# A rearranged front for a hybrid layer kernel: half of the modulation unsplit, the projection begun on four channel blocks

## The reference

```python
mod = silu(cond) @ w_ada + b_ada            # 1024 x 6144, one row per token group
shift_a, scale_a, gate_a, shift_f, scale_f, gate_f = split(mod, 6)
h = rmsnorm(x) * norm_mix_g * (1 + scale_a) + shift_a      # x + position embedding for latents
q, k, v, g, za_f, za_b, u = split(h @ w_in)                # 2080 columns
la = log_sigmoid(za @ w_a_up + b_a) / 16                   # rank 16, one per direction
... bidirectional gated linear attention, mean pooling, @ w_out, residual with gate_a
h = rmsnorm(x) * norm_ffn_g * (1 + scale_f) + shift_f
x = x + gate_f * expert_choice_moe(h)                      # 16 experts, 80 rows each
```

## Time and profile before

| what | us |
|---|---|
| median of 3 runs (lowest, highest) | 1917.02 (1916.72, 1923.43) |
| the profiled execution, its own time | 1916.14 |
| its span, first to last instruction | 1914.3 |
| TensorE busy in the span | 1839.0 (96%) |
| VectorE, ScalarE busy | 1559.4, 1257.9 |
| DMA over the span | 326 GB/s |

### The profile page before, as it was taken

One profiled execution on the slowest core, in us unless ns is written; L12 is line 12 of the kernel. 1 busy time (PEld: TensorE's weight loads), 2 busy tenths in 40 slices (PEclk: granted clock), 3 DMA queues, 4 the chain that ended last, 5 costly groups with the idle time before them and its releaser, 6 DMA issues.

```text
span 1914.3 us, 25062 instructions
## 1 busy us (share of the span) xinstructions
PE 1839.0 (96%) x9064; PEld 1506.5 (79%) x9064; DVE 1559.4 (81%) x1254; ACT 1257.9 (66%) x1005; POOL 272.9 (14%) x118
## 2 busy tenths in 40 slices
PE   3899788999999999999999999999999999999998
PEld 2678666758888888888888888888888888888886
DVE  5531855589898989889898989898989898989897
ACT  5342643257777777767676767676767676777774
POOL 1000000010021211212030303030303030303060
PEclk9999998999999999999999999999999999999999
DMA  9422442579999999999999999999999999999993
GB/s 360 138 63 75 155 151 95 186 276 389 388 386 388 385 385 385 371 384 375 384 377 385 369 385 375 387 370 389 370 386 377 384 368 387 374 384 369 391 378 126
DMA packets 281021, 624.61 MB, mean 326 GB/s; under 512 B 12454, under 2 KB 45851, under 8 KB 280987
## 3 DMA queue, kind: packets, MB, share of 16 engines
q1 hardware_dynamic: 273690, 598.75, 85.2%
q0 software_dynamic: 6000, 20.68, 3.7%
q10 hardware_dynamic: 1296, 4.72, 0.6%
HBM read 608.97 MB, written 15.14 MB: 326 GB/s over the span
## 4 chain that ended last, share of the span: by engine, by line
PE 92%; DVE 4%; ACT 2%; DMA 1%; issue 1%; SPq 0%; ACTq 0%; DVEq 0%
PE bank L1728 17%; PE bank L1729 17%; PE bank L1732 17%; PE bank L1758 8%; PE bank L1754 8%; PE bank L1753 8%; PE bank L1349 3%; PE bank L1350 3%; PE bank L1351 3%; PE bank L1738 1%; DMA raw<-in_w_ada 1%; DVE w_lo L907 1%; ACT w_hi L620 1%; PE bank L1382 1%; PE bank L1558 1%
## 5 line engine op out<-in xcount | busy, mean ns | idle before, releaser
L1211 DVE TENSOR_TENSOR w_lo<-raw,w_hi 128x2048 fp32r<-128x2048 f32 x528 | 1197.9, 2289 | 121.5 <-ACT w_hi L807 119.5
L807 ACT CAST w_hi<-raw 128x2048 fp32r<-128x2048 f32 x524 | 998.0, 1914 | 181.0 <-PE bank L1732 104.2
L1728 PE MATMUL bank<-w_hi,xe_hi 128*128 128x512 f32 (+1 forms) x1536 | 573.8, 380 | 0.0
L1729 PE MATMUL bank<-w_hi,xe_lo 128*128 128x512 f32 (+1 forms) x1536 | 563.4, 373 | 0.0
L1732 PE MATMUL bank<-w_lo,xe_hi 128*128 128x512 f32 (+1 forms) x1536 | 380.4, 373 | 0.0
L1728 PEld LDWEIGHTS bank<-w_hi,xe_hi 128*128 128x128 f32 x1536 | 290.0, 189 | 49.5 <-issue 1.7
L1729 PEld LDWEIGHTS bank<-w_hi,xe_lo 128*128 128x128 f32 x1536 | 290.3, 189 | 48.5
L1732 PEld LDWEIGHTS bank<-w_lo,xe_hi 128*128 128x128 f32 x1536 | 273.4, 189 | 51.8
L1754 PE MATMUL bank<-w_hi,hT_lo 128*128 128x512 f32 x700 | 273.0, 390 | 0.0
L1753 PE MATMUL bank<-w_hi,hT_hi 128*128 128x512 f32 x700 | 272.7, 390 | 0.0
L573 POOL DMA_INDIRECT acc_dram<-yrow,idx_s x15 | 43.6, 2909 | 1072.6 <-DVE yrow L1253 1072.6
(11 more groups left out here) (250 smaller groups left out, 1366.5 us busy)
## 6 DMA issues: line engine op xcount, KB each, us to landing
raw<-in_w_e_gate SPq DMA_DIRECT2D x176, 1024.0 KB, 11.3
raw<-in_w_e_up SPq DMA_DIRECT2D x176, 1024.0 KB, 11.5
raw<-in_w_e_down SPq DMA_DIRECT2D x176, 1024.0 KB, 11.1
raw<-in_w_ada SPq DMA_DIRECT2D x20, 1024.0 KB, 5.4
raw<-in_w_in SPq DMA_DIRECT2D x8, 1024.0 KB, 5.3
raw<-in_w_out SPq DMA_DIRECT2D x4, 1024.0 KB, 5.0
ada_raw<-in_w_ada SPq DMA_DIRECT2D x4, 1024.0 KB, 12.1
acc_dram<-x POOLq DMA_DIRECT2D x5, 512.0 KB, 2.9
```

The costliest lines, as they stand in the source:

```text
L807: nc.scalar.copy(hi_slot(j), raw[:, raw_slot(j), :]).then_inc(hi_done, 1)
L1211: nc.vector.tensor_tensor(lo_slot(j), raw[:, raw_slot(j), :], hi_slot(j), ALU.subtract).then_inc(lo_done, 1)
L1728: nc.tensor.matmul(out, xe_hi[:, kk, :], wh[:, k, :], start=kk == 0, stop=False)
L1729: nc.tensor.matmul(out, xe_lo[:, kk, :], wh[:, k, :], start=False, stop=False)
```

## The change

It changes what happens before and in the first column block. Blocks 0 and 2 of w_ada (the first half of shift and of scale) are loaded ahead of everything else, to places of their own, and multiplied without a split, in plain fp32 with the two columns of silu (`ada_unsplit`). The first unit of w_in comes right behind them. Scale and shift for channel blocks 0 to 3 are then enough to start the projection on these; w_ada blocks 1 and 3, split as before, stand between the first four channel blocks, and blocks 4 to 7 follow. The position rows shrink to one table of 8 rows, spread over the tokens by a matmul with a selection matrix, and one table of 128 rows, added as it is. ScalarE's queue loads the identity and three of the vectors. The decay weights' two parts stand side by side in `wza_both`, so that one product with the rounded h gives both; the up-projection gets its rows twice. The diff, cut to its core; in the rest, `hT_hi` and `hT_lo` become two halves of one tensor (`hT_part`), semaphores are shared, and a few counts follow:

```diff
-PRE = [("ada", b, kh) for b in range(ADA_FIRST) for kh in range(2)]
...
+ADA_ORDER = (0, 2, 1, 3)
+PRE = [("ada", b, kh) for b in ADA_ORDER[2:] for kh in range(2)]
...
-WIN0 = len(PRE)
-PRE += [("win", b, kh) for b in range(4) for kh in range(2)]
...
+WIN0 = len(PRE) - 1
+PRE += [("win", b, kh) for b in range(4) for kh in range(2)][1:]
...
-FRONT = 2 * ADA_FIRST
+FRONT_SLOTS = (0, 1, 6, 7)
+FRONT = len(FRONT_SLOTS)
+W0_SLOT = 2
...
-    return n if n < FRONT else (n - FRONT) % PRE_RING
+    return FRONT_SLOTS[n] if n < FRONT else (n - FRONT) % PRE_RING
...
-        pos_sb = at("pos_sb", [P, T_LAT, D], F32, DR + 20 * KB)
+        ada_f = [at(f"ada_f{q}", [P, UNIT], F32, SPL + (q % 2 * SPLIT + q // 2) * UNIT * 4) for q in range(4)]
+        pos_col = at("pos_col", [P, 512], F32, SPL + 40 * KB)
+        pos_row = at("pos_row", [8, 512], F32, SPL + 42 * KB)
+        pos_sel = at("pos_sel", [8, 8, GRID_W], F32, SPL + 44 * KB)
+        w0_hi = at("w0_hi", [P, UNIT], F32R, DR)
+        w0_lo = at("w0_lo", [P, UNIT], F32R, DR + 8 * KB)
...
+        hT_split = at("hT_split", [P, 2, 2, KD // 2, NTOK], F32R, HT)
...
-            for row, v, n in ((V_C, c[0], KD), (V_CCTX, c_ctx, KD), (V_BADA, b_ada[0], 48),
-                              (V_GMIX, norm_mix_g[0], KD), (V_GFFN, norm_ffn_g[0], KD),
-                              (V_GGLA, gla_norm_g[0], 1), (V_PSC, pool_scale[0], 4)):
+            for row, v, n in ((V_C, c[0], KD), (V_CCTX, c_ctx, KD), (V_BADA, b_ada[0], 48), (V_GMIX, norm_mix_g[0], KD)):
                 load(vecs[row:row + n, :], v.rearrange("(k p) -> k p", p=P), vec_in)
-            load(const[:, :], consts, const_in)
+            for q in range(4):
+                b, kh = ADA_ORDER[q // 2], q % 2
+                load(ada_f[q].rearrange("p (k n) -> p k n", k=4), rows(w_ada[0, kh * 512:(kh + 1) * 512, b * 512:(b + 1) * 512]), ada_in[q])
+            load(raw[:, W0_SLOT, :].rearrange("p (k n) -> p k n", k=4), rows(w_in[0, 0:512, WIN_BLOCKS[0]:WIN_BLOCKS[0] + 512]), w0_in)
             for n in range(NPRE):
                 if n >= FRONT:
-                    last = [q for q in range(n) if pre_slot(q) == pre_slot(n)][-1]
-                    sp.wait_ge(lo_done, last + 1)
+                    last = [q for q in range(n) if pre_slot(q) == pre_slot(n)]
+                    if last:
+                        sp.wait_ge(lo_done, last[-1] + 1)
+                    else:
+                        sp.wait_ge(w0_l, 1)
                 load(raw[:, pre_slot(n), :].rearrange("p (k n) -> p k n", k=4), pre_source(n),
                      raw_full[pre_slot(n)])
...
+                    load(const[:, P:K_COLS], consts[:, P:K_COLS], const_in)
...
+            for r in range(0, 4 * RANK, 2 * RANK):
+                pool.dma_start(wup[r:r + RANK, 0:hw], w_a_up_f[0]).then_inc(up_in, 16)
+                pool.dma_start(wup[r + RANK:r + 2 * RANK, hw:2 * hw], w_a_up_b[0]).then_inc(up_in, 16)
...
+                elif u < SPLIT:
+                    act.wait_ge(ada_f_ps, 2)
+                    act.wait_ge(x_pos, T_LAT)
...
+            act.dma_start(const[:, 0:P], consts[:, 0:P]).then_inc(id_in, 16)
+            for row, v, k in ((V_GFFN, norm_ffn_g[0], KD), (V_GGLA, gla_norm_g[0], 1), (V_PSC, pool_scale[0], 4)):
+                act.dma_start(vecs[row:row + k, :], v.rearrange("(k p) -> k p", p=P)).then_inc(vec_in, 16)
+            tokens(0)
+            act.dma_start(pos_row[:, :], pos.rearrange("(r c) d -> r c d", c=GRID_W)[:, 0, 0:512]).then_inc(pos_in, 16)
+            act.dma_start(pos_col[:, :], pos[0:P, 512:D]).then_inc(pos_in, 16)
+            for t in range(1, TILES):
                 tokens(t)
...
+                q = place_of(b)
+                if q < 2:
+                    act.wait_ge(ada_f_ps, q + 1)
+                else:
+                    act.wait_ge(unit_used, ada_unit(b) + 2)
+                    act.wait_ge(mod_ps, q - 1)
+                m = 2 if q < 2 else 4
+                nc.scalar.copy(modrow[0:m, q % 2, :], ada_bank(b)[0:m, :]).then_inc(mod_row, 1)
...
+            square(0)
+            square(1)
+            turned(0)
+            square(2)
+            turned(1)
+            square(3)
+            mod_rows(0)
+            turned(2)
+            square(4)
+            turned(3)
+            act.wait_ge(xT_ps, 2 * T_LAT)
+            act.wait_ge(w0_in, 16)
+            nc.scalar.copy(w0_hi[:, :], raw[:, W0_SLOT, :]).then_inc(w0_h, 1)
+            turned(4)
+            mod_rows(2)
+            high_row(0)
+            high_row(1)
             high(0)
             high(1)
-            square(0)
+            high_row(2)
+            high_row(3)
             high(2)
-            mod_rows(0)
-            square(1)
-            high(3)
-            square(2)
-            high(4)
-            mod_rows(1)
-            square(3)
-            turned(0)
-            high(5)
-            square(4)
-            turned(1)
-            turned(2)
-            high(6)
-            mod_rows(2)
-            turned(3)
-            high(7)
-            high(8)
-            turned(4)
             act.wait_ge(small_in, 48)
             nc.scalar.copy(wza_hi[:, :, 0:2 * RANK], wza[:, :, :]).then_inc(wza_h, 1)
+            nc.scalar.copy(wza_both[:, :, 0:2 * RANK], wza[:, :, :]).then_inc(wza_h, 1)
+            high(3)
+            mod_rows(1)
+            high(4)
             mod_rows(3)
...
+            for k in range(4, KD):
+                high_row(k)
+                if k == 5:
+                    high(5)
...
             def place(t):
-                dve.wait_ge(x_in[t], 32)
-                nc.vector.tensor_tensor(x_all[:, t, :], x_all[:, t, :], pos_sb[:, t, :], ALU.add).then_inc(x_pos, 1)
+                dve.wait_ge(tile_in[t], 16)
+                dve.wait_ge(pos_ps, t + 1)
+                nc.vector.tensor_tensor(x_all[:, t, 0:512], x_all[:, t, 0:512], bank[4 + t % 2 * 2][:, :], ALU.add).then_inc(x_row, 1)
+                dve.wait_ge(pos_in, 32)
+                nc.vector.tensor_tensor(x_all[:, t, 512:D], x_all[:, t, 512:D], pos_col[:, :], ALU.add).then_inc(x_pos, 1)
...
+                at_ = place_of(b)
+                dve.wait_ge(mod_ps, at_ + 1)
+                if at_ >= 1:
+                    dve.wait_ge(mod_done, at_ + (b >= ADA_FIRST))
...
+                if at_ < 2:
+                    nc.vector.tensor_tensor(modT[:, 4 * b:4 * b + 4, :], q[:, :, 0:2], bias, ALU.add).then_inc(mod_done, 1)
+                    return
...
+            dve.wait_ge(id_in, 16)
+            nc.vector.tensor_copy(pos_sel[:, :, :], ident[0:8, 0:8].unsqueeze(2).broadcast_to([8, 8, GRID_W])).then_inc(pos_set, 1)
...
+            def scale_rows(half):
+                ks = slice(4 * half, 4 * half + 4)
+                dve.wait_ge(mod_done, 2 * half + 2)
+                gm = vecT[:, V_GMIX + 4 * half:V_GMIX + 4 * half + 4].unsqueeze(2).broadcast_to([P, 4, 2])
+                nc.vector.scalar_tensor_tensor(out=scaleA[:, ks, :], in0=modT[:, 8 + 4 * half:12 + 4 * half, :], scalar=1.0, in1=gm, op0=ALU.add, op1=ALU.mult).then_inc(
+                    scaled if half == 0 else mod_done, 1)
+                if half == 0:
+                    dve.wait_ge(scaled, 1)
+                else:
+                    dve.wait_ge(mod_done, ADA_FIRST + 1)
...
+            def low_row(k):
+                dve.wait_ge(h_hi, k + 1)
+                nc.vector.tensor_tensor(hT_part(1, k), hT[:, k, :], hT_part(0, k), ALU.subtract).then_inc(h_lo, 1)
+            place(0)
+            norm(0)
+            place(1)
+            norm(1)
+            turned(0)
+            place(2)
+            norm(2)
+            turned(1)
+            place(3)
+            norm(3)
+            turned(2)
+            mod_columns(0)
+            norm(4)
+            turned(3)
+            dve.wait_ge(w0_h, 1)
+            nc.vector.tensor_tensor(w0_lo[:, :], raw[:, W0_SLOT, :], w0_hi[:, :], ALU.subtract).then_inc(w0_l, 1)
+            turned(4)
+            mod_columns(2)
+            scale_rows(0)
+            dve.wait_ge(xT_act, TILES)
+            dve.wait_ge(xT_dve, TILES)
             modulated(0)
-            dve.wait_ge(wza_h, 1)
-            nc.vector.tensor_tensor(wza_lo[:, :, 0:2 * RANK], wza[:, :, :], wza_hi[:, :, 0:2 * RANK], ALU.subtract).then_inc(wza_l, 1)
-            for k in range(KD):
-                if k + 1 < KD:
-                    modulated(k + 1)
-                dve.wait_ge(h_hi, k + 1)
-                nc.vector.tensor_tensor(hT_lo[:, k, :], hT[:, k, :], hT_hi[:, k, :], ALU.subtract).then_inc(h_lo, 1)
-                if k in (3, 6):
-                    low(8 + k // 3)
+            modulated(1)
+            low_row(0)
+            modulated(2)
+            low_row(1)
+            low(0)
+            modulated(3)
+            low(1)
+            low_row(2)
+            low_row(3)
+            low(2)
+            dve.wait_ge(wza_h, 2)
```

(89 more changed lines are left out.)

142 lines of the change are left out of this document (39 added, 103 removed).

## The result

The kernel after takes 1903.08 us (median of 5 runs, 1901.39 to 1907.02), beside 1917.08 us for the kernel before on the same chip (5 runs, 1916.72 to 1923.43). The ratio is 0.9923, with a 95% interval of 0.9906 to 0.9939: faster by 0.6 to 0.9%. The forecast was 1901 us, range 1895 to 1910. The profiled execution took 1903.08 us with a span of 1901.3, 13.0 less than the 1914.3 before.

The account below looks back on a forecast made before the run. TensorE bounds the kernel, so the front adds one for one: first block at 42.6 us, plus 42.4 and 0.9, is 85.9 against 101.7, 15.8 gained; 1916.14 becomes 1900.3, 0.9 up to the median, given as 1901 us, range 1895 to 1910.

Parts of the forecast that it names:

- the front alone decides, and what is behind it keeps its length: Before the second column block: 15.8 us gained; from there to the end the same 1812 us as before.
- rival E: In the experts: the front is shorter but they give it back, total 1917 us; chance 0.04.
- D: In the front: SyncE's units land late, free up to 17.5 us; at 25 us, total 1907; chance 0.05.
- F: In the front: a pause behind each ScalarE table load, three in all, total 1905 us; chance 0.02.
- G: Small loads behind 9.5 MB land late, costing from 54 us on, 1927 at 80; expected landing 39; chance 0.03.
- The wait ahead of channel block 4: In the first column block: TensorE waits 0.8 to 1.1 us for the last scale rows.
- the landing of the column table: In the front: 262 KB, issued at about 3, lands at 7.5 us without a wait; at 11 adds 3.2.
- the first unsplit half: In the front: first half block of unsplit w_ada takes 4.4 us, to 21.9, with 3.3 us at half rate.
- the half rate of the first projection block: In the first column block: half clock adds 1.7 us to a sum of 42.4.
- The 65-row decay weights cost TensorE nothing by rows.: In the up-projection: 512 columns stream whatever the rows are; no cost, bounds 0 and 5 x 1.05 us.

Follow-up runs that it names:

- The run with the tables first: Kernel after with the two small position loads ahead of three vector loads and the first tile of x in ScalarE's queue; median 1901.49 us, ratio 0.9902.
- the other order: Kernel after, small tables kept, with all four places and squares ahead of the first copy to hT; median 1901.76 us, ratio 0.9904.
- pipelined: Kernel after with small tables loaded first and each place issued ahead of the norm of the tile before; median 1897.69 us, ratio 0.9884.
- the warmed kernel: Kernel after with 18 more identity products on TensorE before the position products; median 1904.02 us, ratio 0.9912.
- the kernel with three decay products: Kernel after with the decay rows back in three products and 33 rows; median 1907.30 us, ratio 0.9942.
- the one with full rows: Kernel after with 2.1 MB of position rows loaded again, no position products, all places ahead of the first copy to hT; median 1896.57 us, ratio 0.9890.

## Why the prediction was right, and where it was off

**Right: the front alone decides, and what is behind it keeps its length.** The stages behind 190 us moved as a whole (last rows 1896.7 to 1883.7, 13.0), so rival E, the gain given back by the experts, didn't occur. Neither did D (TensorE waits for no unit of w_ada in the front), F (in the kernel after too silu follows its table load by 0.01 us), nor G: the small loads were issued at 25.48 and took 12.6, landing at 38.1 where I had 39. The wait ahead of channel block 4 was 0.70 us by TensorE's own idle time, and I had given it 0.8 to 1.1.

**Off by 2.2: the landing of the column table.** The step "Issued at about 3 it lands at 7.5 and nobody waits" failed. I took the 5.0 us of the first position load, issued at 1.18. The row is that of the second, issued at 2.14, and says 8.7; the third, issued at 3.34, took 11.4. This 256 KB load, issued at 3.17, took 6.67, while 330 GB/s were moved: ahead of it in its own queue stood 592 KB, and SyncE's first unit was issued at 2.27 where before it was 3.61. My own bound, 3.2 us for a landing at 11, was nearer than the 7.5 of the sum. Place 0 ended its first half at 12.76 in place of about 10.5. The run with the tables first gave 1.8 us back, which shows this cause.

**Off by 1.5: the first unsplit half.** "The first half block takes 4.4" took 5.84 in the chain, since half rate went on for longer than the 3.3 us of the earlier trace rows. I had used one measured duration of a state as if it were a constant, and the trace of before had others, in its own front:

```profile
42.34 1.06 PE L1402 MATMUL bank<-const,xn 128*128 128x128 f32 x8 [2.61 <-ACT hT L643]
...
45.98 1.94 PE L1402 MATMUL bank<-const,xn 128*128 128x128 f32 x8 [2.25 <-ACT hT L643]
```

The eight turns take 1.06 us behind a pause of 2.61 and 1.94 behind a shorter one of 2.25. From 45.98 half rate goes on to 51.34, 5.4 us at a granted clock of 0.51. By 25.7 us I was 3.8 behind, and every later step kept that distance or lost a little of it (28.8 became 32.48, 42.6 became 46.15). Two kernels with an unchanged product give 1.0 of the 1.5 back by a shorter half rate (4.92 us with the other order, 4.89 pipelined). Whether full clock all through would bring the whole 1.5 back was not shown: the warmed kernel lost its clock again before it.

**Off by 0.9: the half rate of the first projection block.** I added 1.7 us for it; by the chain's rows, 13 products and a part took 5.84 us (46.15 to 51.99) where 14 x 0.23 is 3.2, so 2.6. The region was 44.2 long in place of 43.3. (The same sum for the kernel before, given as 36.7, adds up to 36.5; from 65.10 to 101.53 it was 36.43.)

**Off by 1.9 the other way: "The 65-row decay weights cost TensorE nothing by rows."** The bounds that I gave, 0 and 5 x 1.05, pointed upward, and excluded a gain for no reason that the rows gave. The cost was in the trace of before: the product after the one at 104.41 in the earlier trace rows starts 1.05 us behind it, where two unsplit instructions of 0.443 are 0.89, and it is itself 0.32 behind the one ahead (104.09), where 0.23 is usual. I read the 1.05 as the price of the operation, not as a sign that something around it was waiting. The kernel before with nothing but its rows changed (1.8 less), and the same stretch of the kernel with three decay products (1.8 more), show that it hangs on the number of rows.

The Trainium skill (TensorEngine Tiling (Array Packing), Key Properties) says that changing the tiling mode drains TensorE. That fits the pauses on both sides of a 33-row product between 128-row ones, where weights aren't loaded ahead, and none around a 65-row one. No run here shows the mode of a product, so the drain as the cause stays argued.

The terms add up as follows: 15.8 forecast, less 3.5 for the front and 0.9 for the block, plus 1.9, is 13.3; the trace shows 11.2 at the second column block and 1.9 behind it, 13.1, and the span 13.0. By parts, the start on four channel blocks has 6.6 of it and the two-group decay 3.3, both by undoing them. The small tables with their order took 6.0 away. The rest, 9.1, is left for the unsplit first half and its loads by subtraction (13.0 - 6.6 - 3.3 + 6.0); it was not undone by itself, so this figure is not measured, and it holds only as far as the parts add. One part also holds a difference in half rate that isn't explained, 1.0 of the 6.0.

## What to carry to other kernels

In a front where three in-order engines hand tiles to each other, write down the order of one engine and ask of each waiting instruction what stands behind it. Here an order that issues the next tile's sum ahead of this tile's norm, and the table that it needs first in the queue, were worth 6 us together and cost no instruction. A load made smaller saves only where its landing is what is waited for; check that before paying for it with products. Look at the time from one product's start to the next, not at its duration: over the whole tile, a small product here took 0.38 us more than it needed, which its listed 1.12 us (1.02 with 65 rows) doesn't show.

## What the hardware showed that I had not expected

- Thirty-two rows of zeros made a product cheaper: tiles of the up-projection come every 3.63 us with 65 rows (nine kernels) and every 4.01 with 33 (the kernel before and the one with three decay products).
- The half rate at the start of the first block lasted 3.3 us before the change (from 65.10), behind a pause of 3.38, but 5.8 in the kernel after (46.15 to 51.99), 5.0 in the pipelined one and 3.6 in the one with full rows, behind pauses of 3.06 in all three. One measured length isn't a constant.
- The length of the pause didn't tell whether half rate followed: in the kernel before it did behind 2.25 us (45.98) and did not behind 2.61 (42.34) or 2.12 (from 58.87 on, 0.23 us from product to product).
- The granted clock read 1.00 in a stretch whose eight instructions took 5.84 us where they later take 3.60 (19.86 to 25.69), and 0.50 in the warmed kernel for the same instructions at 6.41. It also read 1.00 over the kernel before's first products at 0.43 us (23.3 to 28.0). In the first microseconds of these kernels the durations have to be read.
- A rate won by 18 added products (3.10 in place of 5.48 us) was lost again over a wait of 3.85 us.
